# Four of five input projections of a two-layer encoder as seven block products a pair

## Chip, core and metric

One core of one Trainium2 chip. The metric is the device time of one execution in microseconds (us); the median of three runs stands for the kernel. The profile is of one further execution.

## What is computed

Two layers over 512 tokens of 1024 features, all in float32. Layer 0 has one input projection, whose columns feed a retention part and a gated linear recurrence; layer 1 has another mixer; each layer ends with a mixture of 16 experts. The change touches only the start of layer 0:

```python
proj = (h @ w_in).astype(jnp.float32)            # 512 x 1024 times 1024 x 2560
q, k, v, g, xr, gr = jnp.split(proj, list(EVEN_SPLITS), axis=-1)
ret = _head_norm(_retention_bidir(q, k, v))      # q, k after rotary
ret_out = jax.nn.silu(g) * ret
lru_out = _rglru_bidir(xr, conv_w, ...) * jax.nn.gelu(gr)
y = jnp.concatenate([ret_out, lru_out], -1) @ w_out
```

## The kernel before

The five engines run programs of their own, written out by hand, which meet only at semaphores; there is no planner, and the order of the code is the order of the work on each engine. `sp.dma_start` issues on SP's queue, `act.dma_start` on ScalarE's.

The 2560 columns are five groups of 512 (`W_GROUPS`, line 183): 0 is q and k, 1 is xr, 2 is g, 3 is gr, 4 is v. Each lies in SBUF as eight chunks of 128 rows (`w_grp`). `hT` is x transposed, eight chunks of 128 features by 512 tokens. `project(n)` (line 503) makes one bank of 128 x 512 from eight chunks: for xr and gr the output lies with features on the partitions, for q, k, g and v with tokens. n = 0 to 3 is group 0, and so on to 19. A float32 matmul shows in the trace as two passes. The banks 4 to 7 of PSUM take turns, and a projection waits until the bank's last user has emptied it (`proj_used`, `g_used`).

TensorE's order: projections 0 to 3 with the transposes of x between their chunks (line 490), the parameters' transpose (532), projections 4 to 7 (xr), 16 transposes of q and k (556), projections 8 to 11 (g), 16 gate products (567), projections 12 to 18, then the scores of the retention (581) with the chunks of projection 19 between them, the router's sums (540), scores times values (589), and the output projection of layer 0 (618), which wants `lru_done` and the weights `w_out0` (`wout_in`).

ScalarE copies each projection to SBUF or, for g, takes its sigmoid (lines 1049 to 1058); then the sixteen gate sigmoids (1084), and for each of the two scan directions z the exponentials, tanh and a square root (1093 to 1102). It also issues four transfers that zero the slot rows in memory (1069).

VectorE copies the transposes of x (1334), rotates q and k (1345 to 1350), convolves xr (1381, 1384), works out a chain of small parameter terms (1390 to 1408), copies qkT (1412), multiplies g (1416), and for each z computes the recurrence's inputs (1421 to 1428) and scans (1434). Then it multiplies the scores by the decay (1473), makes the recurrence's output (1439, 1442), and normalises the heads.

GpSimd computes gelu's argument from gr in three steps (1950 to 1954), and after ScalarE's sigmoid of it multiplies gr (1956).

x is loaded once, into `h`, where the residual sum after the output projection (1599) finds it again. The decay table is one transfer on SP between the loads of groups 1 and 2.

Of the kernel before, what the change touches and what calls it, by code (L numbers as in the profile page):

```python
# [19 lines left out]
P = 128  # L20
# [72 lines left out]

def constants():
# [29 lines left out]
def encoder_kernel(nc, x, w_in_even, w_out_even, lru_conv_w, lru_conv_b, lru_gate_w, lru_gate_b,  # L124
# [3 lines left out]
    with ExitStack() as ctx:  # L128
# [53 lines left out]
        gelu_tmp = S3(15888, NT, 512)  # L182
        W_GROUPS = [0, 1536, 1024, 2048, 512]
        w_grp = [W3(4096 * n, ND, 512) for n in range(5)]
        zero, prm_rows = S[:, 17936:18192], S[:, 18192:18320]
# [98 lines left out]
        proj, proj_used, g_sigm, g_used = sem("proj"), sem("proj_used"), sem("g_sigmoid"), sem("g_used")  # L284
# [39 lines left out]

        def places_of(u):

            return sorted({p for p in range(NE) if 4 * u < FIRST_STRIP[p] + STRIPS[p] and FIRST_STRIP[p] < 4 * u + 4})
# [15 lines left out]
        def _(sp):  # L343
# [6 lines left out]
            for n, first in enumerate(W_GROUPS):  # L350
# [128 lines left out]
        def _(pe):  # L479
# [23 lines left out]
            def project(n, chunks=range(ND)):  # L503

                grp, i = n // 4, n % 4
                if i == 0 and n > 0:
                    pe.wait_ge(win_in[grp], 16)
                if n >= 16 and chunks[0] == 0:
                    pe.wait_ge(proj_used, n - 7)
                elif 12 <= n < 16:  # L510
                    pe.wait_ge(g_used, n - 11)
                elif 4 <= n < 12:
                    pe.wait_ge(proj_used, n - 3)
                if n < NT:
                    pe.wait_ge(hT_done, 2 * n + 2)
                for c in chunks:
# [4 lines left out]
                    if grp in (1, 3):  # L521
                        a, b = w_grp[grp][:, c, i * P:(i + 1) * P], hT[:, c, :]
                    else:
                        a, b = hT[:, c, i * P:(i + 1) * P], w_grp[grp][:, c, :]
                    last = pe.matmul(ps[:, 4 + n % 4, :], a, b, start=(c == 0), stop=(c == ND - 1))  # L525
                if chunks[-1] == ND - 1:
                    last.then_inc(proj, 1)

# [21 lines left out]
            for n in range(4, 8):  # L550
                project(n)
# [6 lines left out]
            for n in range(8, 12):  # L558
                project(n)
# [9 lines left out]
            for n in range(12, 19):  # L569
                project(n)  # L570
# [266 lines left out]
            pe.wait_ge(wout_in, 16)  # L837
# [145 lines left out]
            pe.wait_ge(wout_in, 32)  # L983
# [37 lines left out]
        def _(act):  # L1021
# [27 lines left out]
            def projected(n):  # L1049

                grp, i = n // 4, n % 4
                act.wait_ge(proj, n + 1)
                bank = ps[:, 4 + n % 4, :]
                if grp == 2:
                    nc.scalar.activation(g0[:, i, :], bank, ACT.Sigmoid).then_inc(g_sigm, 1)
                else:
                    to = {0: qk[:, i, :], 1: xrp[:, i, 2:2 + T], 3: gr[:, i, :], 4: v0[:, i, :]}[grp]
                    copy(to, bank).then_inc(proj_used, 1)

            for n in range(4):  # L1060
                projected(n)
# [3 lines left out]
            act.wait_ge(zero_set, 1)  # L1065
            unwritten = 1 + MAXX
# [5 lines left out]
            for n in range(4, 8):  # L1072
                projected(n)
# [5 lines left out]
            for n in range(8, 12):  # L1079
                projected(n)  # L1080
# [963 lines left out]
```

## Time and profile before

| | us |
|---|---|
| median of 3 runs | 1268.1 (1268.02 to 1270.9) |
| the profiled execution | 1271.66 |
| its span, first to last instruction | 1269.8 |
| TensorE busy | 1222.9 |
| VectorE busy | 517.8 |
| ScalarE busy | 215.1 |
| GpSimd busy | 175.0 |
| mean granted TensorE clock | 0.989 of full |

In the rows further down PE is TensorE's matmuls, PEld its weight loads, DVE is VectorE, ACT ScalarE, POOL GpSimd, SP SyncE; L525 is line 525 of the kernel; `ps<-W,hT 128*128 128x512 f32 x64` is a tile written from the tiles read, with shapes and the number of instructions. A bracket names the idle time before, and what ended it. Matmuls overlap, so a run's busy time has the drain of its last one in it (some 0.15 us), which the chain's pieces have not. "issue" is time in which an engine waited for nothing that the profile shows.

### The profile page before, as it was taken

The numbers are of one execution on the slowest core, as the hardware profiler recorded it, in microseconds if no ns is written. First come the engines' busy times: TensorE is split into PE (matmuls) and PEld (weight loads), VectorE is DVE, ScalarE is ACT, GpSimd is POOL, SyncE is SP. The second block draws the span as 40 slices with busy tenths as digits, with TensorE's granted clock in tenths as the row PEclk, the third lists the DMA queues.
The fourth block names the chain that finished last, engine by engine and source line by source line (L and its number), as shares of the span: only waits on it lengthen the run. The fifth ranks groups of instructions, "written<-read, shape, count | busy, mean of one in ns | idle before, by whom it ended". The sixth has DMA issues, their size and how long they took to land.

```text
span 1269.8 us, 13915 instructions
## 1 busy us (share of the span) xinstructions
PE 1222.9 (96%) x5487; PEld 564.9 (44%) x5487; DVE 517.8 (41%) x1022; ACT 215.1 (17%) x342; POOL 175.0 (14%) x132
## 2 busy tenths in 40 slices
PE   8999989989999998899999999999899899999986
PEld 4444455443333333344555555555454433333332
DVE  1532775472311111710454655565535723111107
ACT  0016501110000000111222122212212200000002
POOL 0000310002200002000122332233210013000013
PEclk9999999989999999999999999999999899999999
DMA  9900038289999999553221122200036799999994
GB/s 354 366 1 0 1 137 337 89 314 399 407 430 425 427 428 413 201 147 133 67 67 29 38 67 66 53 13 1 1 132 298 298 377 397 428 425 429 426 424 173
DMA packets 77825, 292.62 MB, mean 230 GB/s; under 512 B 6500, under 2 KB 46280, under 8 KB 64840
## 3 DMA queue, kind: packets, MB, share of 16 engines
q1 hardware_dynamic: 60464, 257.31, 51.2%
q0 software_dynamic: 4896, 17.83, 3.6%
q10 hardware_dynamic: 12408, 16.67, 3.6%
q8 instruction: 43, 0.70, 0.2%
q14 instruction: 14, 0.11, 0.0%
HBM read 269.24 MB, written 22.54 MB: 230 GB/s over the span
## 4 chain that ended last, share of the span: by engine, by line
PE 82%; DVE 9%; DMA 6%; issue 1%; ACT 1%; DVEq 0%; SPq 0%
PE ps L712 20%; PE ps L893 15%; PE ps L525 9%; PE ps L749 9%; PE ps L618 8%; PE ps L915 4%; PE ps L880 4%; DMA W<-moe_w_down 3%; DMA S<-moe_w_down 3%; PE ps L945 2%; PE ps L769 1%; PE ps L668 1%; PE ps L589 1%; DVE S L1866 1%; PE ps L933 1%
## 5 line engine op out<-in xcount | busy, mean ns | idle before, releaser
L712 PE MATMUL ps<-W,S 128*64 128x512 f32 (+1 forms) x1200 | 272.6, 593 | 3.6 <-DMA W<-moe_w_up 1.7
L893 PE MATMUL ps<-hT,W 128*128 128x512 f32 x512 | 232.5, 593 | 0.7 <-ACT W L1023 0.7
L712 PEld LDWEIGHTS ps<-W,S 128*64 128x64 f32 (+1 forms) x1200 | 81.6, 123 | 133.9 <-issue 130.6
L712 PE MATMUL ps<-S 128*32 128x512 f32 (+1 forms) x592 | 140.2, 593 | 0.5 <-DVE S L1780 0.5
L893 PEld LDWEIGHTS ps<-hT,W 128*128 128x128 f32 x512 | 92.8, 191 | 90.4 <-issue 88.5
L749 PE MATMUL ps<-W,hT 128*64 128x512 f32 (+1 forms) x512 | 116.2, 601 | 5.3 <-DMA S<-moe_w_down 2.2
L2003 POOL TENSOR_TENSOR W<-S,sq 128x256 f32<-128x256 f32 x64 | 73.5, 1149 | 160.8 <-PE ps L915 117.0
L1023 ACT ACTIVATE hT<-ps 128x512 f32<-128x512 f32 x68 | 39.1, 597 | 319.2 <-PE ps L749 235.4
L749 PE MATMUL ps<-S,hT 128*32 128x512 f32 (+1 forms) x384 | 87.8, 602 | 1.0 <-DVE hT L1807 1.0
L525 PE MATMUL ps<-W,hT 128*128 128x512 f32 x192 | 87.0, 609 | 0.8 <-DVE hT L1334 0.8
L1961 POOL DMA_INDIRECT S<-token_rows,row_at x18 | 17.4, 968 | 488.6 <-PE ps L668 288.1
L1908 DVE TENSOR_TENSOR S<-S 128x512 f32<-128x512 f32 x64 | 47.8, 748 | 69.6 <-PE ps L915 57.7
L915 PEld LDWEIGHTS ps<-S,W 128*128 128x128 f32 x448 | 61.6, 193 | 30.7 <-issue 30.7
L1798 DVE TENSOR_TENSOR hT<-hT,ps 128x512 f32<-128x512 f32 x20 | 13.7, 685 | 127.8 <-ACT hT L1147 127.8
L915 PE MATMUL ps<-S,W 128*128 128x128 f32 x448 | 63.7, 286 | 1.4 <-issue 0.8
L712 PEld LDWEIGHTS ps<-S 128*32 128x32 f32 (+1 forms) x592 | 40.5, 118 | 45.5 <-issue 44.5
L749 PEld LDWEIGHTS ps<-W,hT 128*64 128x64 f32 (+1 forms) x512 | 34.7, 125 | 56.8 <-issue 55.8
L618 PE MATMUL ps<-S 128*128 128x512 f32 x128 | 58.6, 601 | 1.0 <-DVE S L1846 1.0
L1023 ACT ACTIVATE W<-ps 128x512 f32<-128x512 f32 x56 | 32.9, 603 | 154.8 <-PE ps L912 40.0
L1807 DVE COPY hT<-ps 128x512 f32<-128x512 f32 x20 | 13.8, 691 | 110.3 <-PE ps L738 109.5
L1803 DVE TENSOR_TENSOR hT<-hT,ps 128x512 f32<-128x512 f32 x20 | 13.8, 688 | 110.0 <-PE ps L712 102.9
L525 PEld LDWEIGHTS ps<-W,hT 128*128 128x128 f32 x192 | 36.7, 195 | 47.4 <-issue 46.2
(284 smaller groups left out, 1367.5 us busy)
## 6 DMA issues: line engine op xcount, KB each, us to landing
W<-moe_w_gate SPq DMA_DIRECT2D x22, 2048.0 KB, 17.6
W<-moe_w_up SPq DMA_DIRECT2D x20, 2048.0 KB, 17.1
W<-moe_w_down SPq DMA_DIRECT2D x20, 2048.0 KB, 22.5
S<-moe_w_down SPq DMA_DIRECT2D x12, 2048.0 KB, 22.1
S<-moe_w_up SPq DMA_DIRECT2D x10, 2048.0 KB, 18.3
S<-moe_w_gate SPq DMA_DIRECT2D x8, 2048.0 KB, 17.2
W<-w_in_odd SPq DMA_DIRECT2D x32, 512.0 KB, 6.4
slot_rows<-hT ACTq DMA_DIRECT2D x18, 512.0 KB, 10.8
```

The source lines that it names most:

```text
L525: last = pe.matmul(ps[:, 4 + n % 4, :], a, b, start=(c == 0), stop=(c == ND - 1))
L618: last = pe.matmul(ps[:, k, :], srcT[:, c, t * P:(t + 1) * P], w[:, c, half * 512:(half + 1) * 512], start=(start and c == tiles[0]), stop ...
L712: last = pe.matmul(ps[a:a + n, bank, :], xgT[:, c, a:a + n], home(kind, p)[:, c, :], start=(c == 0), stop=(c == ND - 1))
L749: last = pe.matmul(ps[a:a + n, 2 + half, :], hidT[:, c, a:a + n], home(DOWN, p)[:, c, half * 512:(half + 1) * 512], start=(c == 0), stop=( ...
L880: last = pe.matmul(ps[:, k, :], hT[:, c, t * P:(t + 1) * P], w_v1[c // 4][:, c % 4, (k % 2) * 512:(k % 2 + 1) * 512], start=(c == 0), stop ...
L893: last = pe.matmul(ps[:, f % 2, :], ring[slot][:, f, c, :], hT[:, c, :], start=(c == 0), stop=(c == ND - 1))
L915: last = pe.matmul(o, km[level % 2][:, c * P:(c + 1) * P], mixed(Q2, s, c * P, P), start=True, stop=True)
L945: last = pe.matmul(ps[:, 7, :], vh[:, j, :], attn[:, j, :], start=(j == 0), stop=(j == NT - 1))
L1023: return nc.scalar.activation(o, i, ACT.Copy)
L1908: v.tensor_tensor(q, q, view(src, at + 1, [[2, n], [step - 1, 2], [0, s]]), ALU.mult).then_inc(updated, 1)
L1961: pool.indirect_dma_start(xg[u % 2], None, token_rows, bass.IndirectOffsetOnAxis(ap=row_at[:, u:u + 1], axis=0)).then_inc(xg_in[u % 2], 16)
L2003: pool.tensor_tensor(view(km[level % 2], s, [[4 * s, m], [s, 2], [1, s]]), view(K2, s, [[4 * s, m], [T + s, 2], [1, s]]), view(ones, 0, [[ ...
```

## The change

The groups 1 and 3 (xr, gr) form one pair, 2 and 4 (g, v) the other; the loads are reordered so that the pairs are adjacent, `w_grp[1]`, `w_grp[2]` and `w_grp[3]`, `w_grp[4]`. For a pair, x is cut in two halves of tokens by two of features, the weights of 1024 columns in two halves of features by the two groups. Seven block products, each of depth 512 (four chunks), 256 tokens and 512 columns, give the four quarters of the result, by sums of x's blocks (`x_form`), of the weights' blocks (`w_forms`) and of the products (`SUMS`). Each product fills two banks (b = 0, 1). VectorE makes three sums of x, and a fourth later; four of the weights a pair, 128 x 2048 each; and for each bank of the products one sum of 128 x 512 that reads PSUM (none for the first product, two for the seventh). ScalarE only keeps the first product of each pair (`keep`), then does one sigmoid of g over 128 x 2048 later on, and VectorE multiplies g by it among the decayed scores (`gated`).

The first pair's products have 256 tokens as moving columns, two matmuls a chunk and bank. Pair 0 stands where projections 4 to 7 stood and before the transposes of q and k; then come the gates, and pair 1 takes the place of projections 12 to 19, with four of its chunks left among the scores. The first two weight sums of pair 0 overwrite group 0, those of pair 1 overwrite `h`; so x is loaded a second time, behind `w_out0`, and the output projection waits for both (`wout_in`, 80). The sums of x lie where the second half of the decay table lay, which is loaded after the sixth product of pair 1. The zeroing of the slot rows is issued on SP. GpSimd's steps on gr start after the transposes of q and k and the last sums of pair 0, and its last one waits for the first scan. On VectorE, pair 0 runs: three rotations, three sums of x, the fourth rotation, `weight_forms(0)`, sums of product 1 (both banks), `last_form(0)`, sums of 2, `weight_forms(1)`, sums of 3, the chain of small terms, then the sums of 4 and 5 alternating with the four convolutions, the last sums, and the copies of qkT.

```diff
+PRODUCTS = (1, 2, 6, 7, 4, 3, 5)
+SUMS = {1: ((1, 1), (0, 0)), 2: ((1, 1), (0, 1)), 3: ((0, 1), (1, 1)), 4: ((1, 1), (1, 0)), 5: ((0, 1), (0, 1))}
...
-        gelu_tmp = S3(15888, NT, 512)
-        W_GROUPS = [0, 1536, 1024, 2048, 512]
+        gelu_tmp = S3(0, NT, 512)
+        W_GROUPS = [0, 1536, 2048, 1024, 512]
         w_grp = [W3(4096 * n, ND, 512) for n in range(5)]
+        x_part = [[hT[:, 4 * j:4 * j + 4, 256 * i:256 * i + 256] for j in range(2)] for i in range(2)]
+        x_form = {1: x_part[0][0], 2: x_part[0][1], 3: S3(14096, 4, 256), 4: x_part[1][1],
+                  5: S3(15888, 4, 256), 6: S3(16912, 4, 256), 7: x_part[1][0]}
+        def w_forms(pair):
+            first, second = w_grp[1 + 2 * pair], w_grp[2 + 2 * pair]
+            hf = h[:].rearrange("p t d -> p (t d)")
+            t1, t2 = ((W3(2048 * n, 4, 512) for n in range(2)) if pair == 0 else
+                      (hf[:, 2048 * n:2048 * n + 2048].rearrange("p (n m) -> p n m", n=4) for n in range(2)))
+            return {1: first[:, 0:4, :], 2: first[:, 4:8, :], 3: second[:, 4:8, :], 4: first[:, 4:8, :],
+                    5: t1, 6: t2, 7: second[:, 0:4, :]}
+        def quarter(pair, i, j, b):
+            if pair == 1:
+                return (g0, v0)[j][:, 2 * i + b, :]
+            if j == 0:
+                return xrp[:, 2 * b:2 * b + 2, 2 + 256 * i:2 + 256 * i + 256]
+            return gr[:, 2 * b:2 * b + 2, 256 * i:256 * i + 256]
...
 # SP
-                if n == 1:
-                    sp.dma_start(decay, c_decay).then_inc(tab_in, 16)
+            sp.dma_start(decay[:, 0:2, :], c_decay[:, 0:2, :]).then_inc(tab_in, 16)
             sp.dma_start(gate_w, ...)
-            sp.wait_ge(proj, 20)
+            sp.wait_ge(zero_set, 1)
...
+            for n in range(4):
+                sp.dma_start(zrows[:, n * unwritten:(n + 1) * unwritten, :],
+                             view(zero, 0, [[0, unwritten], [1, 256]])).then_inc(xs_zeroed, 16)
+            sp.wait_ge(proj, made(1, 5, 1))
+            sp.dma_start(decay[:, 2:4, :], c_decay[:, 2:4, :]).then_inc(gatew_in, 16)
+            sp.wait_ge(proj, made(1, 6, 1))
             sp.dma_start(w_out0, w_out_even[0].rearrange(rows, p=P)).then_inc(wout_in, 16)
+            for t in range(NT):
+                sp.dma_start(h[:, t, :], x[0, t * P:(t + 1) * P, :]).then_inc(wout_in, 16)
...
 # TensorE
+            def partial(pair, q, b, chunks=range(4)):
+                p = PRODUCTS[q]
+                xf, wf, bank = x_form[p], w_forms(pair)[p], bank_of(pair, q, b)
+                for c in chunks:
+                    if pair == 0:
+                        for k in range(2):
+                            m = 2 * b + k
+                            last = pe.matmul(bank[:, k, :], wf[:, c, m * P:(m + 1) * P], xf[:, c, :],
+                                             start=(c == 0 and k == 0), stop=(c == 3 and k == 1))
                     else:
+                        last = pe.matmul(bank, xf[:, c, b * P:(b + 1) * P], wf[:, c, :], start=(c == 0), stop=(c == 3))
...
+            def bank_free(pair, q, b):
+                if pair == 0 and q < 2:
+                    pe.wait_ge(proj_used, 2 * q + b + 1)
+                elif q == 2:
+                    pe.wait_ge(proj_used, kept(pair, b))
+                elif q > 2:
+                    pe.wait_ge(added, summed_up(pair, q - 2, b))
+                else:
+                    pe.wait_ge(added, summed_up(0, 5 + q, b))
+            def pair_products(pair, last_bank=True):
+                for q in range(7):
+                    if q == 0:
+                        pe.wait_ge(win_in[1 + 2 * pair], 16)
+                    elif 2 <= q <= 4:
+                        pe.wait_ge(forms_done, 3 * pair + q - 1)
+                    for b in range(2):
+                        if q < 6 or b == 0 or last_bank:
+                            bank_free(pair, q, b)
+                            partial(pair, q, b)
...
-            for n in range(4, 8):
-                project(n)
+            pair_products(0)
             pe.wait_ge(prmC, 1)
...
-            for n in range(8, 12):
-                project(n)
...
-            for n in range(12, 19):
-                project(n)
+            pair_products(1, last_bank=False)
...
             scores(0)
             scores(1)
-            project(19, range(4))
+            bank_free(1, 6, 1)
+            partial(1, 6, 1, (0, 1))
             scores(2)
-            project(19, (4,))
+            partial(1, 6, 1, (2,))
             scores(3)
-            project(19, (5, 6))
+            partial(1, 6, 1, (3,))
             scores(4)
-            project(19, (7,))
             scores(5)
-            pe.wait_ge(proj_used, 16)
+            pe.wait_ge(added, summed_up(1, 6, 1))
...
-            pe.wait_ge(wout_in, 16)
+            pe.wait_ge(wout_in, 80)
...
 # VectorE
+            def weight_forms(pair):
+                wf, b12 = w_forms(pair), w_grp[2 + 2 * pair][:, 0:4, :]
...
+                done(v.tensor_tensor(wf[5], b12, wf[1], ALU.subtract))
+                v.tensor_tensor(wf[6], wf[3], wf[5], ALU.subtract).then_inc(forms_done, 1)
+                if pair == 0:
+                    v.tensor_tensor(x_form[7], x_part[0][0], x_part[1][0], ALU.subtract)
+                v.tensor_tensor(wf[7], wf[3], b12, ALU.subtract).then_inc(forms_done, 1)
+            def last_form(pair):
...
+                v.tensor_tensor(wf[4], wf[2], wf[6], ALU.subtract).then_inc(forms_done, 1)
+            def gather_up(pair, q, b):
...
+                v.tensor_tensor(quarter(pair, *new, b), bank_of(pair, q, b), quarter(pair, *old, b), ALU.add
+                                ).then_inc(added, 1)
+            def gather_last(pair, b):
...
+                for i in range(2):
+                    to = quarter(pair, i, 1, b)
+                    v.tensor_tensor(to, bank_of(pair, 6, b), to, ALU.add).then_inc(added, 1)
...
+            dve.wait_ge(gate_done, 16)
+            inputs(0)
+            squares(0)
+            inputs(1)
+            gather_up(1, 1, 0)
+            scale_inputs(0)
+            gather_up(1, 1, 1)
+            scan(0)
+            gather_up(1, 2, 0)
+            gather_up(1, 2, 1)
+            last_form(1)
+            squares(1)
+            gather_up(1, 3, 0)
+            gather_up(1, 3, 1)
+            gather_up(1, 4, 0)
+            scale_inputs(1)
+            gather_up(1, 4, 1)
+            scan(1)
+            gather_up(1, 5, 0)
+            gather_up(1, 5, 1)
...
 # GpSimd
-            pool.wait_ge(rotated, NT)
-            pool.wait_ge(proj_used, 12)
+            pool.wait_ge(qkT_ps, NT)
+            pool.wait_ge(added, summed_up(0, 6, 1))
...
             pool.wait_ge(gelu_sig, 1)
+            pool.wait_ge(scanned, 1)
             pool.tensor_tensor(gr, gr, gelu_tmp, ALU.mult).then_inc(gelu_done, 1)
```

## Rows read from the trace of the kernel before

**Rows 1.** The page: span; busy time and share of each engine; one group.

```profile
span 1269.8 us, 13915 instructions
...
PE 1222.9 (96%) x5487; PEld 564.9 (44%) x5487; DVE 517.8 (41%) x1022; ACT 215.1 (17%) x342; POOL 175.0 (14%) x132
...
L525 PEld LDWEIGHTS ps<-W,hT 128*128 128x128 f32 x192 | 36.7, 195 | 47.4 <-issue 46.2
```

**Rows 2.** The chain that ended last, in order of time: start us, us, what.

```profile
40.62 27.49 PE ps L525 x64
68.11 1.75 PE ps L556 x16
69.86 27.47 PE ps L525 x64
97.33 13.73 PE ps L567 x32
...
157.86 8.84 DVE W L1434 x4
...
183.16 10.91 PE ps L589 x96
194.08 10.30 PE ps L618 x24
```

**Rows 3.** Timeline of TensorE, 159 to 168 us; in brackets the idle time before.

```profile
159.06 1.99 PE L581 MATMUL ps<-S 64*128 64x512 f32 x8
...
167.93 1.13 PE L581 MATMUL ps<-S 64*128 64x512 f32 x4 [3.25 <-DVE S L1473]
```

**Rows 4.** Windows of 10 us: busy time of the five engines, PEclk, DMA share, GB/s.

```profile
60.00:70.00 10.00, 10.00 (x36) 5.31 (x35) 5.24 (x8) 2.43 (x5) 0.00 (x0) 1.00 0.29 102
...
170.00:180.00 10.00, 10.00 (x57) 4.76 (x57) 4.71 (x10) 1.88 (x2) 0.00 (x0) 1.00 0.35 120
```

**Rows 5.** The chain again, 725 to 735 us.

```profile
731.52 1.73 PE ps L933 x8
```

**Rows 6.** Timeline of VectorE, 38 to 167 us: start us, us, operation.

```profile
38.36 0.42 DVE L1350 TENSOR_TENSOR S<-S 128x256 f32<-128x256 f32 x1
...
69.36 2.33 DVE L1384 SCALAR_TENSOR_TENSOR W<-S,prm,W 128x512 f32<-128x512 f32 x3
...
75.58 2.48 DVE L1412 COPY S<-ps 128x512 f32<-128x512 f32 x4
...
111.82 2.29 DVE L1421 TENSOR_TENSOR W<-W 128x2048 f32<-128x2048 f32 x1 [13.14 <-ACT W L1084]
...
118.41 2.29 DVE L1425 SCALAR_TENSOR_TENSOR W<-W 128x2048 f32<-128x2048 f32 x1 [0.37 <-ACT W L1097]
...
131.01 4.57 DVE L1434 TENSOR_TENSOR_SCAN W<-W 128x512 f32<-128x512 f32 x4
...
147.07 6.49 DVE L1425 SCALAR_TENSOR_TENSOR W<-W 128x2048 f32<-128x2048 f32 x1
...
166.62 3.76 DVE L1473 TENSOR_TENSOR S<-ps,S 128x512 f32<-128x512 f32 x6
```

**Rows 7.** Timeline of ScalarE: one square root of 2048 elements.

```profile
126.74 1.91 ACT L1102 ACTIVATE W<-W 128x2048 f32<-128x2048 f32 x1
```

**Rows 8.** Timeline of GpSimd, 139 to 165 us.

```profile
139.31 3.60 POOL L1950 TENSOR_TENSOR S<-S 128x2048 f32<-128x2048 f32 x1 [138.16 <-ACT S L1023]
...
144.98 6.42 POOL L1954 TENSOR_TENSOR S<-S 128x2048 f32<-128x2048 f32 x1
```

**Rows 9.** Timeline, 1255 to 1260 us: VectorE beside GpSimd.

```profile
1256.49 2.35 POOL L2019 TENSOR_TENSOR h<-h,S 128x1024 f32<-128x1024 f32 x1 [14.36 <-ACT h L1317]
...
1257.21 1.27 DVE L1511 SCALAR_TENSOR_TENSOR h<-ps,sm,S 128x1024 f32<-128x1024 f32 x1
```

**Rows 10.** Windows of 2 us, same columns, during the transfer of w_out0.

```profile
178.00:180.00 2.00, 2.00 (x13) 1.12 (x12) 0.18 (x1) 0.00 (x0) 0.00 (x0) 1.00 1.02 418
```

**Rows 11.** The issue of w_out0: time from issue to landing.

```profile
DMA to landing us min/median/max: 14.2/14.2/14.2
```

More of the change, by code:

```diff
@@ L323, in encoder_kernel, with made, kept, summed_up @@
         block = ctx.enter_context(nc.Block())
+        def made(pair, q, b):
+            return NT + 14 * pair + 2 * q + b + 1
+        def kept(pair, b):
+            return NT + 2 * pair + b + 1
+        def summed_up(pair, q, b):
+            return 14 * pair + (2 * (q - 1) + b + 1 if q < 6 else 10 + 2 * b + 2)
         def places_of(u):
@@ L501, in _, with project @@
             turn_h(0, 0)
[L503 to L516, printed above, removed]
+            def project(n):
+                pe.wait_ge(hT_done, 2 * n + 2)
+                for c in range(ND):
                     if n == 0 and c in (0, 2, 4):
@@ L1047, in _, with keep @@
             act.dma_start(fold[:], c_fold).then_inc(prm_in, 16)
-            def projected(n):
-                grp, i = n // 4, n % 4
+            for n in range(NT):
                 act.wait_ge(proj, n + 1)
[L1053 to L1061, printed above, removed]
+                copy(qk[:, n, :], ps[:, 4 + n, :]).then_inc(proj_used, 1)
             act.wait_ge(prmT, 1)
             copy(prm[:], ps[:, 0, 0:NROWS]).then_inc(prmC, 1)
-            act.wait_ge(zero_set, 1)
-            unwritten = 1 + MAXX
-            zrows = xs[LAST * P:(NU + MAXX) * P, :].rearrange("(p b) (q e) -> p (b q) e", p=P, e=256)
-            for n in range(4):
-                act.dma_start(zrows[:, n * unwritten:(n + 1) * unwritten, :],
-                              view(zero, 0, [[0, unwritten], [1, 256]])).then_inc(xs_zeroed, 16)
+            def keep(pair, b):
+                act.wait_ge(proj, made(pair, 0, b))
+                copy(quarter(pair, 1, 1, b), bank_of(pair, 0, b)).then_inc(proj_used, 1)
             act.wait_ge(zero_set, 2)
-            for n in range(4, 8):
-                projected(n)
+            for b in range(2):
+                keep(0, b)
             act.wait_ge(prm_sub, 1)
@@ L1337, in _, with rotate @@
             pairs = [[DKR, 2 * HR], [2, DKR // 2]]
-            tmp = [view(gelu_tmp, 256 * n, [[DKR // 2, 2 * HR], [1, DKR // 2]]) for n in range(4)]
-            for t in range(NT):
+            tmp = [view(qkT, 256 * n, [[DKR // 2, 2 * HR], [1, DKR // 2]]) for n in range(4)]
+            def rotate(t):
                 dve.wait_ge(proj_used, t + 1)
@@ L1387, in _ @@
                 ins.then_inc(conv_done, 1)
+            for b in range(2):
+                gather_up(0, 1, b)
+            last_form(0)
+            for b in range(2):
+                gather_up(0, 2, b)
+            weight_forms(1)
+            for b in range(2):
+                gather_up(0, 3, b)
             dve.wait_ge(prm_exp, 1)
@@ L1408, in _ @@
             done(v.memset(col("olb", 8, 1), 0.0))
+            gather_up(0, 4, 0)
+            convolve(0)
+            gather_up(0, 4, 1)
+            convolve(1)
+            gather_up(0, 5, 0)
+            convolve(2)
+            gather_up(0, 5, 1)
+            convolve(3)
+            gather_last(0, 0)
+            gather_last(0, 1)
             for t in range(NT):
@@ L1413, in _, with inputs, squares @@
                               ).then_inc(qkT_done, 1)
-            for i in range(NT):
-                dve.wait_ge(g_sigm, i + 1)
-                v.tensor_tensor(g0[:, i, :], g0[:, i, :], ps[:, 4 + i, :], ALU.mult).then_inc(g_used, 1)
-            for z in range(2):
-                dve.wait_ge(gate_done, 16)
+            def inputs(z):
                 v.tensor_tensor(IG[z], IG[z], xc, ALU.mult)
+            def squares(z):
                 dve.wait_ge(a_done, z + 1)
@@ L1428, in _, with scan @@
                 done(v.tensor_tensor(IG[z], IG[z], TMP, ALU.mult))
+            def scan(z):
                 for n in range(LRU_BLOCKS):
```

85 lines of the change are left out of this document (62 added, 23 removed).

## The prediction

> **What bounds the kernel now.** The page first: TensorE is busy for 1222.9 of 1269.8 us, 96% [rows 1]. The others have room over the whole span, but a share over a whole span says nothing of one stretch, so the chain comes next, from 40 to 194 us [rows 2]. Up to 138 us it is TensorE alone: in the rows four projections, transposes of q and k, four projections, sixteen gate products and then four more projections, one after the other without a gap. Four projections of 512 columns take 27.47 us, so one takes 6.87 and one of its eight chunks 0.86. After that the chain runs through VectorE, the second scan taking 8.84 us. What this costs TensorE is seen in its own timeline: one wait of 3.25 us at 167.93, for the decayed scores that stand behind that scan [rows 3]. So to 194 us the time is TensorE's work plus 3.25 us, and the change shortens the one and shifts the other.
>
> **Products.** Each pair replaces eight projections by seven products of half the depth and the doubled width; a product costs a projection's 6.87 us. Of sixteen projections fourteen are left: **-13.74 us**. The first pair's matmuls have 256 columns instead of 512, twice as many. The nearest row is the 256-column product of line 933: eight passes in 1.73 us, 0.216 each [rows 5], half of the 512-column pass (27.47 / 64 = 0.429). So I take the same time per product. The second pair keeps 512 columns.
>
> **First pair, from 40.5 us.** TensorE makes products until 40.5 + 48.1 = 88.6, transposes q and k (1.75) until 90.3, and then waits for qkT and the convolution before the gates. VectorE gets everything in between, priced by its rows [rows 6]: 2.3 us for 2048 elements (2.2 where nothing waits on it), 0.62 for 512 from PSUM (six in 3.76), 2.9 for one block's convolution (three steps in 2.33 and a first one of 0.6), 3.9 for the small chain behind it (71.7 to 75.58), 2.48 for the four qkT copies. It is free of the third rotation at 38.8. The forms of x are three sums of 1024 elements; no row before 200 us has that shape, so I bound one between 0.7 (512 elements) and 2.3 (2048) and take 1.2, the middle by elements: 42.5. The last rotation, six operations of 256 elements at 0.4, takes 2.3: 44.8. The first weight form is ready at 47.1, the second at 49.3, wanted at 40.5 + 13.7 = 54.2; the third at 52.7, wanted at 61.1. So even at the upper bounds (3.3 us later) the third product isn't held. Its last wait is for the third product, at 61.2. From there its own list runs through: one sum 61.8; three weight forms of the second pair 6.7; two sums 1.2; the chain 3.9; four sums 2.5; four convolutions 11.6: 87.7. Then the four sums of the last product, 2.5: 90.2; then qkT, 2.5: 92.7, and a semaphore's 0.1. **The gates start at 92.9, after an idle of 2.6 us that was not there before: +2.6.** It cannot fall below about 2.2, since two sums and the copies follow the last product at 88.7; and each further us on VectorE after 61 us adds one. VectorE lies here without slack: this is the term to watch.
>
> GpSimd's three steps on gr start at 90.4. In this trace VectorE and GpSimd exclude each other when both read two tiles of SBUF: line 1425 took 6.49 instead of 2.29 us beside GpSimd's 6.42 [rows 6, 8]. A VectorE operation with one side in PSUM did not: 1.27 us beside GpSimd's 2.35 [rows 9]. The qkT copies are of that kind, so I add nothing; if they were held, the first step (3.60) would add up to 3.6.
>
> **Second pair.** Gates 13.73 us [rows 2] end at g = 106.7; thirteen half products of 3.44 us end at g + 44.7 = 151.3, where the first scores stood at 159.06 [rows 3]. On VectorE, with the distances of before (inputs at g + 0.8, the ratio at g + 9.6, a root of 1.91) [rows 6, 7]: the ratio's root is ready at g + 11.6; inputs (2.3), a scan of 4.57, and three sums end the first scan at g + 19.9; then GpSimd's last step on gr excludes VectorE until g + 23.6, the fourth form is ready at g + 25.9 against g + 27.5 wanted, the second scan ends at g + 40.1, the sums at g + 42. So nothing is late at g + 44.7, and **the wait of 3.25 us goes: -3.25**. The reserve is 1.6 us at the form and 2.6 at the end.
>
> **Scores to out-projection.** Before, 35.0 us (159.06 to 194.08) with eight chunks of the last projection in it, and the wait. Now four chunks stand there (counted above). VectorE gets four sums and four gate products more, 5 us, behind the scores; walked through in order, with 1.1 us per score [rows 3] and 0.62 per decay or sum [rows 6], the fourth decay is done at +7.8 and score 5 wants it at 9.1; the last sums are done at +9.4 and wanted at 10.2; the list ends at +23.1 against +28 wanted. Nothing waits. Out-projection at 151.3 + 28.2 = 179.5.
>
> **Transfers.** The last product ends at +8.1, 159.4; w_out0 is issued at 159.6, lands after 14.2 us [rows 11] at 173.8, and behind it x again, 2.10 MB at 418 GB/s [rows 10] or 5.0 us: 178.8, against 179.5 wanted. Hidden with 0.7 us to spare: the second place to watch. The Trainium skill ("SBUF — State Buffer", Summary: rules for kernel authors) asks to reckon about 358 GB/s between HBM and SBUF. By it the 6.29 MB of both take 17.6 us, estimated, instead of 15.0, x lands at 181.4, and TensorE waits 1.9 us: 1255.5. The row stands against it, with 418 GB/s in the middle of this very transfer.
> The half of decay that is split off (0.92 MB, some 4 us) is issued at 148 and wanted at 161. Group 2 of the weights leaves in decay's place and so arrives earlier; the zeroing is the last of the early transfers, all are over within the stretch 60 to 70 us, where the mean is down at 102 GB/s [rows 4], and the second pair's forms want their groups, which precede it, at 61.9. The zeroing of the slots moves from ScalarE's queue to SP's, which has nothing due before 148. ScalarE loses 12 of its 20 small copies and sigmoids and has no wait that TensorE sees.
> Behind the out-projection every step, the experts' loads too, hangs on events and not on a clock, so it shifts as a whole.
>
> **Sum:** -13.74 - 3.25 + 2.6 = -14.4; I say -14.5 with the few switches less. The profiled execution (1271.66 us outside, span 1269.8) should come to 1257.2 and 1255.3. Its time stands 3.6 above the median of the runs, 1268.1, which should come to **1253.6**. A measurement of this kernel tells 0.3%, 3.8 us, from nothing; the forecast is four times that.
>
> **Rivals.**
> A. The reload of x is late, because w_out0 or x flows slower. For it: the reserve of 0.7 us; against: the rate of rows 10. If x goes at the pace of w_out0 from issue to landing (4.19 MB in 14.2 us [rows 11], so 7.1 us), it lands at 180.9 and TensorE waits 1.4 us: 1255.0. If the first expert's loads, issued at 174.5, take half of the engines from it on top, it is up to 5 us: 1258.6.
> B. VectorE's list in the first pair is longer (forms whose tiles are strided, sums held by GpSimd). For it: no slack after 61 us. The gates start 2 to 5 us later: 1255.5 to 1258.5.
> C. The second scan is still late, by a GpSimd step that takes 5 or 6 instead of 3.6 us [rows 8]: up to 3.3 us return, 1256.9.
> D. Slower: the first pair's 224 passes of 256 columns don't hide their weight loads. A load takes 0.195 us [rows 1]; fully exposed it is 224 x 0.19 = 42.6 us, 1296. It decides from 14.5 / 224 = 0.065 us per pass. Against it stands the row of line 933 [rows 5], where passes of this very shape follow each other at 0.216 us.
> E. The new idle lowers the granted clock. The wait of 3.25 us was followed by a clock of 1.00 [rows 4], so I give it nothing of its own.
>
> **Chances.** Forecast (1252 to 1255.5) 0.60; A 0.13; B 0.17; C 0.04; D 0.03; no gain to speak of, by several of them at once, 0.03. The range reaches down to 1251.0, if VectorE is quicker than its sum and the switches cost less, and up to 1259.0, which takes in A, B and C. Faster by over 0.3%: 0.94; within 0.3%: 0.03; slower: 0.03.
>
> **What would show it.** Products of the first pair in 48.1 us without a gap; one idle of 2.2 to 3 us before the gates, ended by VectorE's qkT copy; gates at 93; first scores near 151 with no wait in the second pair and none for decayed scores; out-projection near 179.5, released by TensorE's own work and not by the transfer of x. Passes of the first pair further apart than 0.22 us, waits for sums between the products, or a wait on x above 1 us would prove it wrong.

## The result and the profile after

Beside one another on one chip, ten runs each, the changed kernel takes 1263.2 us (1261.46 to 1267.54) and the kernel before 1270.78 (1268.02 to 1275.19): a ratio of 0.9943 with an interval of 0.9927 to 0.9959. It is faster, but by 7.6 us where 14.5 were forecast, and its time lies outside the range. Of the 9.6 us between 1263.2 and the 1253.6 forecast, 2.7 are only that the kernel before came out at 1270.78 here and not at 1268.1; the other 6.9 are a miss of the forecast. The profiled execution took 1264.57 us, with a span of 1262.7.

The first part of the page of the changed kernel, to be read against [rows 1]:

```profile
span 1262.7 us, 14146 instructions
## 1 busy us (share of the span) xinstructions
PE 1209.0 (96%) x5567; PEld 580.4 (46%) x5567; DVE 549.9 (44%) x1062; ACT 211.6 (17%) x332; POOL 172.5 (14%) x132
```

TensorE is busy 13.9 us less than before. That this is near the forecast's -13.74 is luck: from the first product of the first pair to the output projection it is busy 139.58 us where it was 150.19, 10.6 less, since a product at half clock counts as busy for its whole time (2.9 us more, below), and the rest of the difference lies ahead of that stretch (2.1) and behind it (1.2). The span is only 7.1 us shorter, so TensorE stands idle some 7 us longer (53.7 against 46.9), 4.6 of it in the stretch: 7.81 in two idles where there was one of 3.25. Its timeline shows them. From the changed kernel, engine PE; its columns are start, duration and, in brackets, the idle time before with what ended it:

```profile
39.65 14.00 PE L574 MATMUL ps<-hT,W 128*128 128x256 f32 x64
59.43 9.95 PE L574 MATMUL ps<-S,W 128*128 128x256 f32 x32 [5.78 <-DVE W L1418]
69.21 13.98 PE L574 MATMUL ps<-hT,W 128*128 128x256 f32 x64
83.03 13.98 PE L574 MATMUL ps<-S,W 128*128 128x256 f32 x64
96.84 1.91 PE L630 MATMUL ps<-sq,S 128*128 128x128 f32 x16
100.78 14.00 PE L639 MATMUL ps<-W 128*128 128x512 f32 x32 [2.03 <-DVE S L1536]
...
159.34 1.99 PE L652 MATMUL ps<-S 64*128 64x512 f32 x8
...
187.04 10.46 PE L689 MATMUL ps<-W,hT 128*128 128x512 f32 x24
```

Two products of 256 columns take 14.00 us with their drain, so one takes 6.9, as forecast. No wait is left behind the gates: the 3.25 us of [rows 3] are gone. The idle before the gates is 2.03 us, where 2.6 were forecast. But the third product begins after an idle of 5.78 us, waiting for VectorE's line 1418, the second weight form; and the product itself takes 9.95 us instead of about 7. Neither stands in the forecast. The windows around it (us, busy time and number of instructions for each engine, granted clock, share of DMA time, GB/s) tell the second apart:

```profile
50.00:55.00 5.00, 3.65 (x17) 2.86 (x16) 4.90 (x10) 0.00 (x0) 0.00 (x0) 1.00 1.05 354
55.00:60.00 5.00, 0.57 (x1) 0.50 (x2) 4.96 (x3) 0.00 (x0) 0.00 (x0) 0.83 1.04 343
60.00:65.00 5.00, 5.00 (x13) 3.99 (x12) 4.96 (x9) 1.71 (x3) 0.00 (x0) 0.50 0.49 165
65.00:70.00 5.00, 5.00 (x24) 4.37 (x24) 2.73 (x3) 0.00 (x0) 0.00 (x0) 0.99 0.00 0
```

From 60 to 65 us TensorE ran 13 matmuls where it ran 24 in the next 5 us: a granted clock of 0.50, the lower of its two levels (1.2 in place of 2.4 GHz). It fell during the idle: it was 1.00 up to 58 us, 0.63 from 58 to 59 and 0.50 from 59 on, and the product began at 59.43.

Why VectorE was late is found by following it back. Its timeline in the changed kernel:

```profile
42.16 0.42 DVE L1405 TENSOR_TENSOR S<-S,rot 128x256 f32<-128x256 f32 x1 [10.99 <-DMA S<-c_decay]
...
54.76 2.29 DVE L1417 TENSOR_TENSOR W<-W 128x2048 f32<-128x2048 f32 x1
57.08 2.29 DVE L1418 TENSOR_TENSOR W<-W 128x2048 f32<-128x2048 f32 x1
...
95.72 2.61 DVE L1447 TENSOR_TENSOR S<-ps,S 128x512 f32<-128x512 f32 x4
98.25 2.48 DVE L1536 COPY S<-ps 128x512 f32<-128x512 f32 x4
...
136.02 5.45 DVE L1428 TENSOR_TENSOR W<-W,h 128x2048 f32<-128x2048 f32 x1
```

and the chain of waits of the same kernel around it (start, us, what):

```profile
24.55 17.59 DMA S<-c_decay
42.14 0.02 issue
42.16 0.42 DVE S L1405
...
57.08 2.30 DVE W L1418
59.39 0.04 issue
59.43 37.59 PE ps L574 x160
```

The first rotation of q and k, which reads `S` and `rot` and nothing of the decay table, waits 10.99 us for the transfer of the decay table. The reason is in the code: VectorE's `dve.wait_ge(tab_in, 64)` in front of the rotations asks for four transfers counted on one semaphore (the rotation table, the router's weights, iota, and decay). Before, decay left between the groups 1 and 2; the change sends its first half behind all groups. It is issued at 24.55, lands at 42.14, and everything on VectorE stands behind it. In the kernel before, the last of the four had landed at 26.2 us (iota; decay at 20.9), and the first rotation, at 31.89, waited for none of them.

### The profile page after: what moved, and what is told of

Its sections match the earlier page's. It is cut to its first block, busy times and chain, and to the rows that moved or that the text cites. A ratio compares the mean times of both kernels' runs of the same rounds, so it can differ in the third digit from the quotient of the medians.

```text
span 1262.7 us, 14146 instructions
## 1 busy us (share of the span) xinstructions
PE 1209.0 (96%) x5567; PEld 580.4 (46%) x5567; DVE 549.9 (44%) x1062; ACT 211.6 (17%) x332; POOL 172.5 (14%) x132
## 3 DMA queue, kind: packets, MB, share of 16 engines
q1 hardware_dynamic: 67904, 266.22, 53.7%
## 4 chain that ended last, share of the span: by engine, by line
PE 76%; DVE 10%; DMA 9%; SPq 2%; issue 2%; ACT 1%; DVEq 0%; POOLq 0%
PE ps L783 18%; PE ps L964 15%; PE ps L820 8%; PE ps L689 8%; DMA W<-moe_w_up 4%; PE ps L577 4%; PE ps L986 4%; PE ps L951 4%; PE ps L574 3%; DMA S<-moe_w_down 3%; PE ps L1016 2%; PE ps L840 2%; SPq L401 2%; DMA S<-c_decay 1%; PE ps L739 1%
## 5 line engine op out<-in xcount | busy, mean ns | idle before, releaser
L820 PE MATMUL ps<-W,hT 128*64 128x512 f32 (+1 forms) x512 | 114.6, 597 | 3.7 <-DMA S<-moe_w_down 1.6
L951 PE MATMUL ps<-W,hT 128*128 128x512 f32 x128 | 56.0, 594 | 1.1 <-ACT hT L1094 0.7
L689 PE MATMUL ps<-W,hT 128*128 128x512 f32 x128 | 55.9, 592 | 0.0
```

What stands on the lines that cost most here:

```text
L689: last = pe.matmul(ps[:, k, :], srcT[:, c, t * P:(t + 1) * P], w[:, c, half * 512:(half + 1) * 512], start=(start and c == tiles[0]), stop ...
L820: last = pe.matmul(ps[a:a + n, 2 + half, :], hidT[:, c, a:a + n], home(DOWN, p)[:, c, half * 512:(half + 1) * 512], start=(c == 0), stop=( ...
L951: last = pe.matmul(ps[:, k, :], hT[:, c, t * P:(t + 1) * P], w_v1[c // 4][:, c % 4, (k % 2) * 512:(k % 2 + 1) * 512], start=(c == 0), stop ...
```

## Experiments

The theory from here: **the shared count is the one cause of the miss.** Rivals: (R1) the idle is not from the count but from VectorE's list, whose order puts rotations before forms; (R2) the slow third product is a property of these passes (strided forms, transfers beside them) and not of the clock after an idle; (R3) the later transfer costs the kernel in other ways too. Because TensorE's first product starts 1 to 2 us earlier or later from one execution to the next, the runs are compared by the stretch **from the first product of the first pair** (in the kernel before, projection 4) **to the output projection**: 193.91 - 40.46 = 153.45 before, 187.04 - 39.65 = 147.39 after, and 179.5 - 40.5 = 139.0 in the forecast. The stretch is read from one profiled execution of each kernel; the medians and ratios are of several. A ratio is always to the kernel before, run beside it on the same chip.

**1. A count of its own.** The decay half is sent at the same place, but counted with the gate weights, so that the rotations wait for three tables alone (the last `wait_ge` on `tab_in` below; the router's two waits on that semaphore go down by 16 too). The gates and the decayed scores wait for the longer count.

```diff
-            sp.dma_start(decay[:, 0:2, :], c_decay[:, 0:2, :]).then_inc(tab_in, 16)
+            sp.dma_start(decay[:, 0:2, :], c_decay[:, 0:2, :]).then_inc(gatew_in, 16)
...
-            pe.wait_ge(gatew_in, 16)
+            pe.wait_ge(gatew_in, 32)
...
-            dve.wait_ge(tab_in, 64)
+            dve.wait_ge(tab_in, 48)
...
-                    if m == NT:
-                        dve.wait_ge(gatew_in, 32)
+                    if m % NT == 0:
+                        dve.wait_ge(gatew_in, 32 + 4 * m)
```

> The changed kernel with one thing altered: the first half of the decay table is counted by gatew_in and no longer by tab_in, on which the rotations wait. Theory S (the shared count: the rotations, which need only the rotary table, waited for the decay table that now lands behind four weight groups; all of VectorE's list came 10 us late): rotations start near 31, the third product follows the second without idle time (5.8 us gone), no stretch at half clock (2.9 us gone), idle before the gates 2.0 to 2.6 us, output projection near 178.5, so 8 us under the changed kernel and 14 to 15 under the kernel before. Theory L (VectorE's list is too long for the pair whatever its start): the idle before the third product stays above 3 us. Theory W (the weight groups themselves land late): the same.

Measured: 1255.38 us (1253.01 to 1259.58) against 1273.0 for the kernel before, ratio 0.9856 (0.9839 to 0.9872). TensorE's timeline:

```profile
40.73 14.00 PE L574 MATMUL ps<-hT,W 128*128 128x256 f32 x64
54.57 7.07 PE L574 MATMUL ps<-S,W 128*128 128x256 f32 x32
...
93.03 14.00 PE L639 MATMUL ps<-W 128*128 128x512 f32 x32 [2.02 <-DVE S L1536]
...
179.30 6.17 PE L689 MATMUL ps<-W,hT 128*128 128x512 f32 x14
```

VectorE's first rotation, in the same kernel:

```profile
32.16 0.41 DVE L1405 TENSOR_TENSOR S<-S,rot 128x256 f32<-128x256 f32 x1
```

The decay half is issued at 24.6 and lands 17.3 us later, at 41.9, as late as before the edit; but the rotations now start at 32.16, without a wait. No idle before the third product, and that product takes 7.07 us; gates at 93.03 (forecast 92.9); output projection at 179.30 (forecast 179.5). The stretch is 138.57 us. A second time on another chip, where the gates were slow as told below:

> The kernel with the own count again, on the same chip as the one whose gates start at once, to tell them apart: 0.9856 of the kernel before.

Measured: 1256.23 us (1254.37 to 1259.57), ratio 0.989 (0.9861 to 0.9918), stretch 140.26. A count of its own takes the whole of the miss away, though the transfer is as late as ever.

**2. The table back in its old place**, still half of it and on the shared semaphore.

```diff
                 else:
                     sp.dma_start(w_grp[n], src).then_inc(win_in[n], 16)
-            sp.dma_start(decay[:, 0:2, :], c_decay[:, 0:2, :]).then_inc(tab_in, 16)
+                if n == 1:
+                    sp.dma_start(decay[:, 0:2, :], c_decay[:, 0:2, :]).then_inc(tab_in, 16)
```

> The changed kernel with the first half of the decay table issued where it was, between the groups 1 and 2, and counted as in the changed kernel. Theory S: rotations start when it lands, near 21 us plus 5, at the latest 32, so the same time as with its own count, within 1 us, although group 2 now lands 2 us later. Theory W: group 2 later means the first weight sum later, so slower than the kernel with its own count by about 2 us.

Measured: 1257.1 us, ratio 0.9873 (0.985 to 0.9897); the table lands at 22.8, the rotations start at 31.16 with no wait, no idle before the third product, stretch 140.26. Position or count, either takes the miss away: they are one cause. The 1.7 us more than in the first run lie in the gates.

**3. The same delay in the kernel before** (R3): decay behind all groups there.

```diff
-                if n == 1:
-                    sp.dma_start(decay, c_decay).then_inc(tab_in, 16)
+            sp.dma_start(decay, c_decay).then_inc(tab_in, 16)
```

> The kernel before with its decay table issued behind all weight groups, nothing else. Theory S: rotations start near 45 instead of 32, but TensorE wants q and k only at 68, so no more than 0.3% from the kernel before: the late table costs only where the weight sums stand behind the rotations. Rival: the late table is bad for other reasons (its transfer collides), then this is slower by several us as well.

Measured: 1269.7 us, ratio 0.9982 (0.9964 to 1.0001); the stretch grew from 153.45 to 155.08, and that by the clock, which was 1.00 up to 167 us and 0.50 from 167 to 170:

```profile
159.77 3.70 PE L524 MATMUL ps<-W,hT 128*128 128x512 f32 x8
166.71 1.84 PE L580 MATMUL ps<-S 64*128 64x512 f32 x4 [3.23 <-DVE S L1472]
168.47 2.07 PE L524 MATMUL ps<-W,hT 128*128 128x512 f32 x2
170.47 1.13 PE L580 MATMUL ps<-S 64*128 64x512 f32 x4
```

The first rotation started at 43.86, after 13.08 us of waiting for the table, and TensorE shows no idle before its transposes of q and k at 66.75. There late rotations cost nothing: before those transposes TensorE needs nothing that VectorE makes from the rotations on. So R3 falls, and a late table has its price only with the new products: it is not the delay but what stands behind it that changed.

**4. Idle or clock** (R2): the changed kernel with TensorE kept at work in front of the third product by eight matmuls of 384 columns, whose results are not used.

```diff
+                    if pair == 0 and q == 2:
+                        spin(3, 8)
```

> The changed kernel with eight 384-column matmuls on constant data (5.1 us at full clock) put between the second and the third product, where TensorE stood idle 5.8 us. They compute nothing that is used. If the stretch at half clock is due to that idle, the granted clock stays at 1.00, the third product takes 6.9 instead of 9.8 us and the kernel is 2.9 us faster than the changed kernel, though nothing was brought forward. Rival: the third product is slow because its operands are just written, then it still takes 9.8 us.

Measured: 1260.47 us, ratio 0.9897 (0.988 to 0.9914). TensorE's timeline:

```profile
54.28 5.32 PE L548 MATMUL ps<-sq 128*128 128x384 f32 x16
59.49 7.17 PE L574 MATMUL ps<-S,W 128*128 128x256 f32 x32
66.50 13.98 PE L574 MATMUL ps<-hT,W 128*128 128x256 f32 x64
```

The third product starts when it did before (59.49 against 59.43) beside the same transfers, and takes 7.17 in place of 9.95 us. So R2 falls: the 2.8 us are the clock after an idle, and they come back although VectorE's form is as late as ever. Nor is it that the operands were just written, the expectation's own rival, since they were here too. The whole stretch became only 1.55 us shorter (145.84), since this time the gates ran slow (15.70 us for 14.00). The ratio fell by more, by 5 to 6 us against the changed kernel's 0.9943, on a chip on which the changed kernel itself was not run; that surplus isn't explained, and nothing here rests on it.

**5. The order of VectorE's list** (R1): the changed kernel with its shared count, but the sums of x and the first pair's weight forms ahead of the rotations.

```diff
-            dve.wait_ge(tab_in, 64)
...
-            for t in range(NT - 1):
-                rotate(t)
+            dve.wait_ge(hT_done, 2 * NT)
...
-            rotate(NT - 1)
...
+            dve.wait_ge(tab_in, 64)
+            for t in range(NT):
+                rotate(t)
```

> The changed kernel with its late, shared count left alone, but the sums of x and the weight forms of the first pair in front of the rotations. Theory S (lateness of the first weight forms, not the table's transfer, is what TensorE pays for): third product at once, no stretch at half clock; the rotations now stand at 48 to 58 and VectorE's list ends later, so the gates start near 94.2 (idle 3.8) against 93.0 with the own count and 100.8 in the changed kernel. So 6 to 7 us under the changed kernel, 1 to 2 over the own count. Theory W (transfers themselves): nothing gained.

Measured: 1256.21 us, ratio 0.9879 (0.9862 to 0.9897); no idle before the third product, 2.49 us before the gates, where 3.8 us were expected; stretch 140.73. So R1 is no second cause but a second cure: the miss needs both the late table and the rotations ahead of the forms. With the forms first the late table holds nothing at all: it lands at 42.2, and VectorE comes to the rotations only at 47.60, without a wait. So less delay is left before the gates than expected. Of the 140.73 us some 1.7 are again slow gates (15.70 us).

**6. The last idle.** The forecast holds that VectorE lies without slack, and that two sums and the copies of qkT set a floor. First the chain of small terms, 3.9 us, was put behind the copies, with the count of the first experiment:

```diff
                 gather_up(0, 3, b)
-            dve.wait_ge(prm_exp, 1)
-            done(v.tensor_scalar(col("w"), col("lam"), 2.0, None, ALU.add))
...
                               ).then_inc(qkT_done, 1)
+            dve.wait_ge(prm_exp, 1)
+            done(v.tensor_scalar(col("w"), col("lam"), 2.0, None, ALU.add))
...
```

> Own count, and only the chain of small terms (3.9 us of VectorE) moved behind the copies of qkT. My prediction said VectorE's list is without slack from 61 us on, one us for one. If so, this gains up to 0.4 us at the gates only, since the last sums wait for the last product at 89.1: gates at 92.8 to 93.0. If the list was truly late, the gates start more than 1 us earlier.

Measured in one run: 1252.61 us, stretch 138.57, the idle unchanged. VectorE's timeline of this kernel:

```profile
85.12 1.29 DVE L1447 TENSOR_TENSOR S<-ps,S 128x512 f32<-128x512 f32 x2
88.57 1.29 DVE L1447 TENSOR_TENSOR S<-ps,S 128x512 f32<-128x512 f32 x2 [2.16 <-PE ps L574]
89.78 2.47 DVE L1516 COPY S<-ps 128x512 f32<-128x512 f32 x4
```

With 3.9 us less in front of it VectorE waits 2.16 us for TensorE's last product, and the gates start no earlier. So the idle of 2.02 us is the floor that the forecast named and put at about 2.2: two sums and four copies behind the last product, with the transposes beside them.

Then, with the count of the first experiment too, q and k were transposed between the fifth and the sixth product (`turn_qk`, on TensorE), ScalarE copied qkT, and the small terms followed VectorE's last sums:

```diff
+                    if pair == 0 and q == 5:
+                        turn_qk()
...
+            for t in range(NT):
+                act.wait_ge(qkT_ps, t + 1)
+                copy(qkT[:, :, t * P:(t + 1) * P], ...).then_inc(qkT_done, 1)
```

> The decay table on its own count, and three moves against the idle before the gates: q and k are transposed between the fifth and sixth product of the first pair, ScalarE copies qkT, and the chain of small terms stands behind the last sums. If the wait before the gates is made only of work that follows the last product (two sums, four copies), the gates start 0.1 us after it: idle 2.0 gone, gates near 90.9 where they were at 93.0 with the own count alone, output projection near 177.2, and 2.0 to 2.5 us less time. Rival: VectorE's list is what holds the gates (the last convolution late), then 1 us or more of idle stays.

Measured: 1252.35 us (1251.19 to 1252.91) against 1271.96, ratio 0.9847 (0.9832 to 0.9863). TensorE runs through:

```profile
75.05 1.91 PE L598 MATMUL ps<-sq,S 128*128 128x128 f32 x16
76.79 13.98 PE L574 MATMUL ps<-S,W 128*128 128x256 f32 x64
90.61 13.90 PE L644 MATMUL ps<-W 128*128 128x512 f32 x32
```

The stretch is 136.28 us. On the chip of the second run of experiment 1:

> The kernel whose gates start at once, beside the own count on one chip. In the traces the output projection starts 2.3 us earlier after the first product; if nothing gives it back, the median is 2.0 to 2.5 us below the own count's (0.0016 to 0.0020 of the ratio); if the time behind the output projection swings by more than that, the two intervals overlap.

Measured: 1251.4 us (1249.43 to 1256.36), ratio 0.9857 (0.9827 to 0.9887), stretch again 136.28. By its stretch this version is 2.3 us shorter than the first run of the version with only a count of its own, and 4.0 us shorter than the second, 1.7 of it the clock. By whole times it is 4.8 us below that version on the one chip where both ran, with intervals that overlap; its ratios, 0.9847 and 0.9857, can't be told from the 0.9856 of experiment 1's first run, so that it is the faster of the two rests on the stretch. It is some 19.5 us below the kernel before on either chip, and beats both kernels.

**7. The changed kernel again**, for how well its idle and its clock repeat:

> The changed kernel itself, beside the others on one chip, as the measure for them: 0.994 of the kernel before. The gate products (14.0 us in its profile) may take 15.7 here, as they did in two of the four runs so far after an idle of the same 2 us.

Measured: 1263.83 us, ratio 0.9937 (0.9921 to 0.9952); an idle of 6.71 us and a third product of 9.74, stretch 148.11.

**8. How near is the reload of x?** The version of experiment 1 with three more loads of 1.05 MB ahead of x, into tiles that are free then, and the first expert's loads held until x has landed. SP's wait for the second scan cost nothing: the spare loads were issued at 159.72, right behind `w_out0`.

```diff
+            sp.wait_ge(scanned, 2)
+            for spare in (A_, IG[0], IG[1]):
+                sp.dma_start(spare, x[0]...[:, :, 0:512]).then_inc(wout_in, 16)
             for t in range(NT):
                 sp.dma_start(h[:, t, :], x[0, t * P:(t + 1) * P, :]).then_inc(wout_in, 16)
...
+            sp.wait_ge(wout_in, 128)
             load_expert(0, 0)
```

> Own count, with 3.15 MB more to load (half of x, three times, into tiles that are free by then and not used) ahead of the reload of x, and the first expert's loads held behind them. The prediction gave the reload of x 0.7 us to spare; in the kernel with the own count it lands near 177.2, TensorE wants it at 179.3. At 416 GB/s the addition takes 7.6 us, so x lands near 184.8 and the output projection idles 5.5 us, and then works at half clock for a while (2 to 3 us more). If the reload had no say at all, nothing changes. Whole: 5 to 9 us above the own count.

Measured in one run: 1263.78 us. TensorE's timeline and the windows of this kernel:

```profile
186.61 12.90 PE L693 MATMUL ps<-W,hT 128*128 128x512 f32 x24 [7.61 <-DMA h<-x]
```

```profile
175.00:180.00 5.00, 4.00 (x36) 3.81 (x35) 4.79 (x25) 0.42 (x2) 0.00 (x0) 1.00 1.06 392
180.00:185.00 5.00, 0.00 (x0) 0.00 (x0) 4.75 (x24) 0.41 (x2) 0.00 (x0) 0.61 0.93 371
185.00:190.00 5.00, 3.39 (x4) 1.50 (x5) 3.94 (x11) 0.00 (x0) 0.00 (x0) 0.50 0.53 163
```

The output projection, wanted at 179.0, waits 7.61 us for x, where 5.5 were expected, and 24 of its matmuls then take 12.90 instead of 10.46 us: again half clock behind an idle, 2.4 us. The added 3.15 MB took SP 9.52 us to issue, and at the 381 GB/s that these windows average up to 185 us they would take 8.3. So without them, and with the expert's loads still held, x would have landed 0.7 to 1.9 us before it was wanted, by estimate. In the kernels themselves less is left, as SP's timeline in experiment 1 and the view of that line show:

```profile
160.18 2.39 SPq L415 DMA_DIRECT2D h<-x  x4
175.02 0.33 SPq L429 DMA_DIRECT2D W<-moe_w_gate  x1
DMA to landing us min/median/max: 14.4/15.4/17.0
```

The last quarter of x, issued at 161.9, took the 17.0 us and landed at 178.9, 0.4 us before the output projection began; in the changed kernel it was 169.6 + 17.2 = 186.8 against 187.04, 0.2 us. There the first expert's loads, issued at 175.02, run beside x; that they make up the difference to the estimate is likely but not shown. So the transfer was hidden, but with next to nothing to spare.

## Why the prediction was wrong, by its own steps

| term | forecast | measured |
|---|---|---|
| two products of 256 columns | 13.74 us | 14.00 with the drain of 0.15 |
| idle before the third product | 0 | **5.78, again 6.71** |
| third product | 6.87 | **9.95, again 9.74** |
| idle before the gates | 2.6 | 2.03 |
| wait at the decayed scores | gone | gone |
| GpSimd's last step | 3.6 | 4.54 |
| fourth form of the second pair ready | g + 25.9 | g + 26.9 |
| x landed before it was wanted | 0.7 | 0.2, in experiment 1 0.4 |
| output projection, with the miss / without | 179.5 | 187.04 / 179.30 |

**The step that failed** is the start of VectorE's list: "It is free of the third rotation at 38.8", and with it "The first weight form is ready at 47.1, the second at 49.3". The times were taken from the trace of before, where the first three rotations follow VectorE's copies without a wait. In the part on transfers decay's first half is not followed at all; "Group 2 of the weights leaves in decay's place and so arrives earlier" sees what comes forward and not what goes back. No row warned of it, since in the trace of before all four transfers had landed by 26.2, and the first rotation, at 31.89, waited for none: a wait that is already met leaves no mark, though the program still depends on it. The second form came at 59.39 instead of 49.3.

The sum of the miss, by the stretch: 139.0 forecast, +5.8 for the idle, +2.9 for the third product at half clock (9.95 less 7.07), -0.6 for the gates' idle, and 0.3 left, to 147.4. (The -0.6 is not a better start of the gates: in experiment 1 they start 52.30 us behind the first product, where 52.4 were forecast; TensorE's own work before them took 0.3 us longer, and its drain counts as busy.) The forecast's last 0.1 us, for "the few switches less", has no row behind it, but it is too small to matter. In whole times: 1253.6 forecast from 1268.1 is a ratio of 0.9886; with the count mended the runs gave 0.9856 and 0.989, on either side of it.

**What held.** The products: 256 columns cost half of 512, and the weight loads stayed hidden, so D is out. The floor before the gates: the copies of qkT, with one side in PSUM, took 2.48 us beside GpSimd's step and were not held. The second pair has no wait, but it came near to one. The fourth form, beside GpSimd's last step, took 5.45 us:

```profile
134.77 4.54 POOL L2123 TENSOR_TENSOR S<-S 128x2048 f32<-128x2048 f32 x1 [25.74 <-DVE W L1563]
```

as the mutual exclusion of [rows 6, 8] says. But the step took 4.54 us for the 3.6 that the forecast gave it, so the form was ready at 141.47, 26.9 us behind the gates' end at g = 114.6, and TensorE wanted it at g + 27.5: 0.6 us to spare where the forecast had 1.6. C did not happen, and its price for the step was nearer than the sum's.

**A**, the reload of x, did not happen, but the forecast's 0.7 us to spare were 0.4 in the first experiment, where `w_out0` was issued at 159.76 (forecast 159.6), x landed at 178.9 (forecast 178.8) and the output projection began at 179.30 with no wait. The Trainium skill ("SBUF — State Buffer", Summary: rules for kernel authors) asks to reckon with about 358 GB/s, and by it the forecast had x land at 181.4. The trace disagrees: its windows from 165 to 175 us show 406 to 416 GB/s, and the measurement decides.

**B** is the rival that came nearest: VectorE was late for the third product. But its mechanism, a longer list, is not what happened: with the table in time VectorE's list had no excess at all, since the idle is 2.02 us with the chain of small terms in front of the copies and without it. Nor had it slack to speak of: in experiment 5, with the rotations later, the idle was 2.49.

**E** was given nothing, by the one case in the trace of before in which 3.25 us of idle were followed by a full clock. That was too little evidence. After an idle of 5.78 us the lower level cost 2.9 us, after 7.61 it cost 2.4; after one of 2.0 us it cost nothing in the changed kernel (twice) and in three other profiles, but 1.7 us in four with 2.0 to 2.5 us. One of 3.23 us in experiment 3 cost 1.6. Why it is so with one idle and not with another is not settled here.

The tail behind the output projection was not touched: from its start to the end of the span it takes 1075.9 us before, 1075.7 after, 1078.4 in the first and 1073.6 in the fastest version, with a mean granted clock of 0.987 to 0.989 in all four. Where the clock was 0.993 (experiment 5) it took 1070.3. These differences are as large as some of the effects above, which is why the stretch decides between versions; the whole times show that each version beats the kernel before, and only roughly by how much.

## What to carry to other kernels

When a change moves a transfer in its queue, look up which semaphore it counts on and who waits for that count: a count that several transfers share makes every waiter wait for all of them, and a trace in which they had all landed in time shows no wait at all. Follow back the engine that a new scheme leans on to its very first wait, since all its times are relative to that. And price an idle of TensorE above its length: here about half as much again came on top of one of 5.8 us, a third on top of one of 7.6, and on top of those of 2 to 3.3 us either nothing or about 1.7 us.

## What the runs showed of the hardware

The same idle is not always followed by the same clock. Before the gates, in the version with a count of its own, 2.02 us of idle stood twice on different chips, once with gates of 14.00 and once of 15.70 us. Windows of the second run, from 90 to 95 and to 100 us:

```profile
90.00:95.00 5.00, 3.60 (x6) 1.58 (x7) 1.34 (x3) 1.38 (x2) 4.91 (x2) 0.75 0.01 3
95.00:100.00 5.00, 5.00 (x12) 2.16 (x11) 0.00 (x0) 3.34 (x5) 4.58 (x2) 0.91 0.00 0
```

and of the first:

```profile
90.00:95.00 5.00, 2.98 (x15) 1.78 (x14) 2.98 (x5) 0.69 (x1) 3.82 (x2) 1.00 0.01 3
95.00:100.00 5.00, 5.00 (x13) 2.13 (x12) 0.00 (x0) 4.09 (x6) 4.92 (x2) 1.00 0.00 0
```

The changed kernel's gates took 14.00 us in both of its profiles after such an idle, and those of experiments 2 (2.02 us), 4 (2.28) and 5 (2.49) took 15.70. The length of the idle alone doesn't decide it. In the kernel before, an idle of 3.25 us left the clock at 1.00, and in experiment 3 one of 3.23 us at the same place was followed by 3 us at 0.50. The idles of 5.8 us and more were followed by half clock in each of three cases.
